# Second attention of a two-block network: values as the stationary operand, two heads in the two column halves, three outputs turned by the product itself

## The reference

```python
# 8 query heads over 2 key/value groups, three branches added with sigmoid gates
o_cmp = softmax(q @ kc.T + bias) @ vc      # 31 compressed blocks
o_slc = selected_attention(q, ks, vs, ...) # all blocks are selected at 512 tokens: full causal
o_win = banded_attention(q, kw, vw, window=512)               # causal too
o_a = g[..., 0:1] * o_cmp + g[..., 1:2] * o_slc + g[..., 2:3] * o_win
# 8 more heads over 2 groups, window 128, with a sink in the softmax
o_b = banded_attention(q_b, k_b, v_b, window=128, sinks=sinks)
x = x + concatenate([o_a, o_b], axis=-1) @ w_out
```

## Time and profile before

| | |
|---|---|
| median of 3 runs | 1645.12 us |
| span of the profiled execution | 1643.2 us |
| around its span, against the median | 1.9 us |
| second attention, first transpose to end of the output projection | some 1041 to 1271 us of the span |
| TensorE busy | 1623.6 us, 99% |
| VectorE, ScalarE, GpSimd busy | 701.2, 674.6, 759.2 us |
| granted TensorE clock | 1.00 in every stretch shown, its level of 2.4 GHz |

### The profile page before, as it was taken

The page is one execution under the profiler, slowest core; times in us unless marked ns, Lnnn a source line. Parts: engine busy times, 40 slices in busy tenths (PEclk is TensorE's granted clock), DMA queues, the critical chain, the costliest instruction groups (busy, mean ns, idle before and its releaser), DMA issues.

```text
span 1643.2 us, 21043 instructions
## 1 busy us (share of the span) xinstructions
PE 1623.6 (99%) x8100; PEld 1349.0 (82%) x8100; DVE 701.2 (43%) x1404; ACT 674.6 (41%) x1183; POOL 759.2 (46%) x581
## 2 busy tenths in 40 slices
PE   9999999999999999999999999999999999999997
PEld 7787888888888888888888888888888888888886
DVE  7276747874444227322113225555773311112224
ACT  6356645543334325422223224567563422223322
POOL 7424454564445552744445552543114544444550
PEclk9999999999999999999999999999999999999999
DMA  5411102323222231323232322212002222223221
GB/s 205 148 52 52 52 1 103 129 90 103 92 101 95 97 101 61 116 96 102 90 103 90 103 92 101 91 66 78 27 27 96 97 94 99 99 94 103 90 103 51
DMA packets 42115, 147.35 MB, mean 90 GB/s; under 512 B 4768, under 2 KB 5152, under 8 KB 42016
## 3 DMA queue, kind: packets, MB, share of 16 engines
q1 hardware_dynamic: 40680, 143.39, 25.7%
q10 hardware_dynamic: 1336, 2.63, 0.5%
HBM read 142.84 MB, written 3.41 MB: 89 GB/s over the span
## 4 chain that ended last, share of the span: by engine, by line
PE 82%; DVE 2%; issue 1%; ACT 1%; POOL 1%; DMA 0%; DVEq 0%; ACTq 0%; POOLq 0%
PE PS L587 20%; PE PS L589 20%; PE PS L588 20%; PE PS L1210 5%; PE PS L548 4%; PE PS L1221 3%; PE PS L1019 2%; PE PS L556 2%; PE PS L977 2%; PE PS L1012 1%; POOL w_lo L645 0%; DVE L L1110 0%; DMA stage<-in_weights 0%; PE PS L609 0%; ACT sq L1057 0%
## 5 line engine op out<-in xcount | busy, mean ns | idle before, releaser
L645 POOL TENSOR_TENSOR w_lo<-stage,w_hi 128x512 fp32r<-128x512 f32 x522 | 707.9, 1380 | 819.2 <-ACT w_hi L619 818.3
L619 ACT ACTIVATE w_hi<-stage 128x1024 fp32r<-128x1024 f32 x262 | 274.8, 1056 | 519.9 <-DMA stage<-in_weights 516.0
L587 PE MATMUL PS<-H_hi,w_hi 128*128 128x512 f32 x992 | 386.1, 389 | 0.4 <-DVE rcol L1407 0.4
L588 PE MATMUL PS<-H_lo,w_hi 128*128 128x512 f32 x992 | 386.0, 389 | 0.0
L589 PE MATMUL PS<-H_hi,w_lo 128*128 128x512 f32 x992 | 385.9, 389 | 0.0
L587 PEld LDWEIGHTS PS<-H_hi,w_hi 128*128 128x128 f32 x992 | 186.2, 188 | 39.0 <-DVE rcol L1407 0.7
L589 PEld LDWEIGHTS PS<-H_hi,w_lo 128*128 128x128 f32 x992 | 186.2, 188 | 38.9
L588 PEld LDWEIGHTS PS<-H_lo,w_hi 128*128 128x128 f32 x992 | 186.2, 188 | 38.7
L587 PE MATMUL PS<-A_hi,w_hi 128*128 128x512 f32 x528 | 205.6, 389 | 0.3 <-DVE A_lo L756 0.3
L589 PE MATMUL PS<-A_hi,w_lo 128*128 128x512 f32 x528 | 205.4, 389 | 0.0
L588 PE MATMUL PS<-A_lo,w_hi 128*128 128x512 f32 x528 | 205.4, 389 | 0.0
(11 more groups left out here) (234 smaller groups left out, 2048.2 us busy)
## 6 DMA issues: line engine op xcount, KB each, us to landing
stage<-in_weights SPq DMA_DIRECT2D x262, 512.0 KB, 3.2
out_t<-Y SPq DMA_DIRECT2D x8, 256.0 KB, 2.0
X<-in_x_t SPq DMA_DIRECT2D x3, 512.0 KB, 8.8
bias_line<-bias_line ACTq DMA_DIRECT2D x1, 1270.0 KB
strip<-bias_line ACTq DMA_DIRECT2D x1, 1024.0 KB, 5.0
stage<-in_weights SPq DMA_DIRECT2D x2, 256.0 KB, 4.6
V<-QF SPq DMA_DIRECT2D x4, 128.0 KB, 2.3
V<-QF SPq DMA_DIRECT2D x4, 127.8 KB, 2.4
```

The lines of the kernel that those rows point to most:

```text
L587: pe.matmul(out, a, h_hi, start=first, stop=False, skip_group_check=skip)
L588: pe.matmul(out, a, h_lo, start=False, stop=False, skip_group_check=skip)
L619: act.activation(w_hi[:, slot, :], stage[:, slot, :], ACT.Copy).then_inc(hi_done, 1)
L645: lo = pool.tensor_tensor(w_lo[:, slot, cols], stage[:, slot, cols], w_hi[:, slot, cols].bitcast(F32), ALU.subtract)
```

## The change

It concerns the second attention and its output projection only.

- The reciprocal (and the gate) multiplies the weights W before they are turned, as one `tensor_scalar` over 128 x nk in place of the 128x1 product with the gate and of the scaling of the result. The transposes of an item now wait for it.
- The values (128 keys x 64) are the stationary operand and the turned weights (128 keys x 128 queries) the moving one. The product comes out with features on the partitions; the heads of items n and n+1 go to partitions 0 to 63 and 64 to 127 of one bank, that is to the two column halves of the array. The two branches accumulate in PSUM. `soft_heads` does both heads at every odd step, two steps later than before.
- `O` becomes flat (`dve_heads_out`, `act_sum_hi` and `dve_sum_lo` for p < 4, `act_heads_hi` and `dve_heads_lo` for p >= 4): the product of four blocks of queries is copied once for each block (128x128) for p < 4, and split straight from PSUM into T_hi and T_lo for p >= 4. The 32 transposes of `O` go. The compressed branch uses the same form.
- The turned weights have four buffers instead of two, transposes two banks instead of three, the product one.
- The rows of the output projection's weights are permuted in pairs of 64, so each of its eight units is loaded by four DMAs with runs of 512 bytes in place of one.
- The filler table changes at its end, and the order of the projection's outputs.

```diff
-TURN_ORDER = [..., [0, 1, 2, 3, 4, 6, 5, 7]]
+TURN_ORDER = [..., list(range(8))]
+WO_ORDER2 = [6, 7, 0, 1, 2, 3, 4, 5]
 FILL2 = [4] * 48 + [6] * 4 + [0] + [6] * 4 + [0] + [3] * 8 + [0] + [3] * 8 + [0] + [3] * 8
-FILL2 = FILL2 + [(0, 4), 0] + [(0, 4), (3, 0)] * 5 + [(3, 12), (12, 6), 6]
+FILL2 = FILL2 + [0, 0] + [4, 3] * 5 + [1] + [6, 6, 6]
...
-                                 out=O[:, i, bass.ts(h, HD)], add=(branch == 1),
+                                 out=PS[g * HD:(g + 1) * HD, HEADS_PS, bass.ts(i, P)], add=(branch == 1),
...
-        return ITEM_PS + it.n % 3
+        return ITEM_PS + it.n % (2 if it.kind == "soft" else 3)
...
+            def soft_heads(n):
+                it = items[n]
+                if not it.add and n > 0:
+                    pe.wait_ge(a.o_done, 4 * it.group + it.i)
+                pe.wait_ge(a.wt_ready, n + 2)
+                blocks = it.nk // P
+                for kb in range(blocks):
+                    for x in (it, items[n + 1]):
+                        mm = pe.matmul(x.out, x.v[kb], turned_weights(x)[:, bass.ts(kb, P)],
+                                       start=(kb == 0 and not x.add),
+                                       stop=(kb == blocks - 1 and (x.add or x.gate is None)))
+                mm.then_inc(a.pv_done, 1)
...
-                        pe.wait_ge(a.comb if it.kind == "diff" else a.exp_done, it.exps)
-                    if it.n >= 3:
+                        pe.wait_ge(a.comb, it.exps)
+                    if it.kind == "soft":
+                        if it.n >= 2:
+                            pe.wait_ge(a.wt_ready, it.n - 1)
+                    elif it.n >= 3:
                         pe.wait_ge(a.o_done, it.n - 2)
...
-                if n >= 3:
+                if a is at2:
+                    if n >= 5 and n % 2 == 1:
+                        soft_heads(n - 5)
+                elif n >= 3:
...
                         c = link(dve.reciprocal(it.st[:, 6:7], it.st[:, 4:5]))
                         after(c)
-                        if it.gate is not None:
-                            c = link(dve.tensor_scalar(it.st[:, 6:7], it.st[:, 6:7], it.gate, None, ALU.mult))
-                            after(c)
-                        dve.sem_inc(a.comb, 1)
+                        w = W[:, it.n % 2, 0:it.nk]
+                        if it.gate is None:
+                            dve.tensor_scalar(w, w, it.st[:, 6:7], None, ALU.mult).then_inc(a.comb, 1)
+                        else:
+                            dve.tensor_scalar(w, w, it.st[:, 6:7], it.gate, ALU.mult, ALU.mult).then_inc(a.comb, 1)
...
+        def act_heads_hi(p, i, pair):
...
+                act.wait_ge(at2.pv_done, pair + 1)
...
+                act.activation(T_hi[:, p, bass.ts(i, P)], PS[:, HEADS_PS, bass.ts(i, P)], ACT.Copy).then_inc(heads_hi, 1)
...
+        def dve_heads_lo(p, i):
...
+                dve.wait_ge(heads_hi, 4 * (p - 4) + i + 1)
+                dve.tensor_tensor(T_lo[:, p, cols], PS[:, HEADS_PS, cols], T_hi[:, p, cols].bitcast(F32),
+                                  ALU.subtract).then_inc(at2.o_done, 1)
...
-                for h in (2 * pair, 2 * pair + 1):
-                    mm = pe.matmul(PS[:, 7, bass.ts(h % 2, 256)], cmp_PT(h), vc4[:, bass.ts(h // 4, 256)], start=True, stop=True)
+                for i in range(TB):
+                    for g in range(2):
+                        mm = pe.matmul(PS[g * HD:(g + 1) * HD, 7, bass.ts(i, P)], vc4[:, bass.ts(4 * g + i, HD)],
+                                       cmp_PT(4 * g + pair), start=True, stop=True)
...
+        for p in range(8):
+            for i in range(TB):
+                last = groups2[p] + (4 * i + 2 if p < 4 else 2 * i)
+                if p < 4:
+                    hook(at2, "dve", last + 6, dve_heads_out(p, i, last // 2))
+                else:
+                    hook(at2, "act0", last + 6, act_heads_hi(p, i, last // 2))
+                    hook(at2, "dve", last + 6, dve_heads_lo(p, i))
...
+            def load_by_pair(u):
+                there = stage[:, u % RING, :].rearrange("p (h j l o) -> p h j l o", h=2, j=2, l=2)
+                here = weights[ORDER[u]].rearrange("p (h g j o) -> p h g j o", h=2, g=2, j=2)
+                for g in range(2):
+                    for l in range(2):
+                        sp.dma_start(there[bass.ts(g, HD), :, :, l, :],
+                                     here[bass.ts(l, HD), :, g, :, :]).then_inc(loaded[u % RING], 16)
```

More of the change, by code:

```diff
@@ L124, in unit_order @@
     order += [U_MIX + (17 + CMP_AT[name] if name in CMP_AT else MIX_AT[name]) for name in FILL2_TASKS]
-    return order + [U_WO2 + j for j in WO_ORDER] + list(range(U_UP3, N_UNITS))
+    return order + [U_WO2 + j for j in WO_ORDER2] + list(range(U_UP3, N_UNITS))
 MIX_AT = {n: i for i, n in enumerate(("q0", "q1", "q2", "q3", "ks", "kw", "kc", "vc",
@@ L152 @@
 NAT_BANK = [4, 5, 7, 2]
-TURN_ORDER = [[c if kind == "diff" else 4 + c for kind, c in GROUPS1], [0, 1, 2, 3, 4, 6, 5, 7]]
+TURN_ORDER = [[c if kind == "diff" else 4 + c for kind, c in GROUPS1], list(range(8))]
 FILL2 = [4] * 48 + [6] * 4 + [0] + [6] * 4 + [0] + [3] * 8 + [0] + [3] * 8 + [0] + [3] * 8
-FILL2 = FILL2 + [(0, 4), 0] + [(0, 4), (3, 0)] * 5 + [(3, 12), (12, 6), 6]
+FILL2 = FILL2 + [0, 0] + [4, 3] * 5 + [1] + [6, 6, 6]
 def fill2_steps(name):
@@ L425, in build @@
         n_mix = Norm("mix", 6, "fold", X)
-        n_ffn2 = Norm("ffn2", 7, "fold", X, order=WO_ORDER)
+        n_ffn2 = Norm("ffn2", 7, "fold", X, order=WO_ORDER2)
         n_final = Norm("final", 8, "final", X)
@@ L612, in pe_token_unit, with loads_of @@
             m.then_inc(unit_done, 1)
+        def loads_of(u):
+            return u // RING + 1 + 3 * sum(1 for v in range(U_WO2, min(u + 1, U_UP3)) if v % RING == u % RING)
         def act_hi(act, u):
@@ L872, in build @@
                              v=[V[:, 0, k0 // P + kb, 2 * P + g * HD:2 * P + (g + 1) * HD] for kb in range(nk // P)],
-                             out=O[:, i, T + h * HD:T + (h + 1) * HD], add=False, gate=None,
+                             out=PS[g * HD:(g + 1) * HD, HEADS_PS, bass.ts(i, P)], add=False, gate=None,
                              sink=row[:, ROW_SINK + h:ROW_SINK + h + 1])
@@ L881, in build @@
                 it.bank = [(it.map0 + m) % 3 for m in range(len(it.maps))]
-                it.dv = it.out.shape[-1]
+                it.dv = HD if it.kind == "soft" else it.out.shape[-1]
                 it.st = stat[:, n % 4, :]
@@ L988, in ahead @@
                 return n < len(items) and n % 2 == 0 and items[n].kind == "sb" and items[n].i in (1, 2)
-            for n in range(len(items) + 3):
+            def soft_heads(n):
[10 more added lines that the diff above has]
+                mm.then_inc(a.pv_done, 1)
+            for n in range(len(items) + (4 if a is at2 else 3)):
                 f = per_item[n] if n < len(per_item) else 0
@@ L1026, in act_attn @@
             items = a.items
-            for n in range(len(items) + 2):
+            for n in range(len(items) + (6 if a is at2 else 2)):
                 for what in a.hooks["act0"].get(n, []):
@@ L1070, in dve_attn @@
             items = a.items
-            for n in range(len(items) + 4):
-                if n >= 4:
+            for n in range(len(items) + (6 if a is at2 else 4)):
+                if n >= 4 and a is at1:
                     it = items[n - 4]
@@ L1075, in dve_attn @@
                     pv = PS[:, item_bank(it), 0:it.dv]
-                    if it.kind == "soft" and it.add:
-                        dve.wait_ge(a.o_done, it.n)
-                        dve.scalar_tensor_tensor(out=it.out, in0=pv, scalar=it.st[:, 6:7], in1=it.out,
-                                                 op0=ALU.mult, op1=ALU.add).then_inc(a.o_done, 1)
-                    elif it.kind != "sb":
+                    if it.kind == "diff":
                         dve.tensor_scalar(it.out, pv, it.st[:, 6:7], None, ALU.mult).then_inc(a.o_done, 1)
@@ L1290, in pe_wo_rest @@
                 pe.wait_ge(lo_done, (U_WO, U_WO2)[b] + at + 1)
-                if WO_ORDER[at] == 3:
+                if b == 0 and WO_ORDER[at] == 3:
                     pe.wait_ge(a.o_done, 1 + max(it.n for it in a.items if item_bank(it) == 3))
                 run(pe_wo1(pe, b, at, range(6)))
-                run(pe_turn1(pe, b, at + 3))
+                if b == 0:
+                    run(pe_turn1(pe, at + 3))
             for g in (6, 7):
@@ L1671, in load @@
                         wait_unit(sp, u - RING)
-                    sp.dma_start(stage[:, u % RING, :], weights[ORDER[u]]).then_inc(loaded[u % RING], 16)
+                    if U_WO2 <= u < U_UP3:
+                        load_by_pair(u)
+                    else:
+                        sp.dma_start(stage[:, u % RING, :], weights[ORDER[u]]).then_inc(loaded[u % RING], 16)
+            def load_by_pair(u):
[5 more added lines that the diff above has]
```

(1 more changed line is left out.)

161 lines of the change are left out of this document (100 added, 61 removed).

## The result

The changed kernel took 1652.15 us (median of 4 runs, 1651.5 to 1654.31) against 1645.06 before (1644.98 to 1645.23): a ratio of 1.0045, interval 1.0033 to 1.0058. It is slower by 7.1 us where 9.3 us less were forecast, and lies above the range. Its profiled execution has a span of 1649.7 us.

The account below looks back on a forecast made before the run. The prediction took TensorE's own pace to bound the kernel. Its terms, -19.9 + 6.7 + 1.5 - 3.5 - 1.2 + 5.8 + 1.3 = -9.3 us, took 1645.1 to 1635.8 us, range 1628 to 1646.

Parts of the forecast that it names:

- The products with the values: Second attention: 432 records in 216 overlapping column-half pairs at 0.11 us, 43.7 us falling to 23.8, so 19.9 us saved.
- the changes of form: Second attention: one more switch of TensorE's array form, 48 times at 0.14 us, costing 6.7 us (4.8 to 11).
- rival (a): Products with the values: the column halves take turns, products cost 47.5 us, kernel 1655.5 us; chance 0.07.
- rival (c): Products with the values: weight loads not hidden behind matmuls in flight, 12 us more, 1647 us less some stalls; chance 0.03.
- The compressed branch: Its products with the values stay at 0.88 us each time, but two changes of form add 1.5 us.
- The transposes of O: The 32 transposes of O on TensorE go, at 0.11 us each, saving 3.5 us.
- the loads in four parts: Output projection: four DMA issues in place of one land the seventh unit later, stalling TensorE 1.3 us (0 to 4).
- the scaling ahead of its turn: Second attention: transposes of an odd item wait for VectorE's scaling; with the related stalls, 5.8 us (2 to 14).
- steps 84 and 85: Second attention: these steps have no filler to cover the wait for the scaling, costing about 1.0 us.
- The zeros of the filler table: Second attention: steps 57, 66 and 75 have no filler to cover the scaling, some 0.3 us each, 1.0 us.
- The place of GpSimd's windows: Second attention, where ScalarE waited 3.06 us for GpSimd's windows: TensorE comes earlier there, so 1.0 us more wait shows.
- Rival (b): Second attention: the VectorE and ScalarE chain binds all 48 pairs, 0.3 us more each, 1646 us, no change; chance 0.11.

Follow-up runs that it names:

- The later logits: Against the changed kernel, TensorE's logits of a pair stand behind the step's first filler and the scaling of the item two before; scaling stays in SBUF: 1661.1 us.

## Why the prediction was wrong

It placed TensorE as the bound and asked whether the other engines could follow: the right question, answered wrongly for one instruction.

- **The products with the values** were forecast at -19.9 with full overlap, and the changes of form at +6.7, together -13.2. Measured by starts, the value records fall from 47.1 to 30.8 us, and the filler ahead of each of 48 groups stands 0.10 us longer (1071.96 to 1072.29 above, 0.33 for 0.227), so about -11.5. The mechanism was right, and rival (a), turns, and rival (c), loads unhidden, fell: a pair costs 0.11 us. The compressed branch, forecast at +1.5, measured about +1.7 by starts.
- **The transposes of O** (-3.5) measured -3.4; the loads in four parts (+1.3) about +1.8; steps 84 and 85 (1.0) showed a wait of 1.2 us.
- **The failed step is the scaling ahead of its turn**, +5.8 on record, bounds 2 and 14. Taking the scaling away gave 16.7 us, and the kernel without it still has 5.0 us of waits at its place in the order, which belong to the same term: some 22 us, an estimate from the two. The forecast less its 5.8 would be 1630.0 for that kernel, and it took 1635.49.
- **What the term lacked: GpSimd**, 10.3 us, of which 0.9 are waits for w_lo. The price per instruction, 0.29 us, came from a row without GpSimd beside it. That row is of the very form that can be held up, and cheaper than this one even alone (0.41 us for 256 columns with a factor and a gate). The earlier trace rows has GpSimd busy 29.4 of 69 us in the same stage, and the prediction used that column for nothing.
- **What the term had too small**: its own length, with the windows, 6.3 us, and the order, 5.0. The zeros of the filler table were counted at steps 57, 66 and 75; the one at step 52 was left out, and TensorE waits 1.1 us there. The place of GpSimd's windows was put at 1.0 and has 1.5 without the scaling, 3.5 with it. Even without GpSimd's subtractions the kernel took 1641.8 us, 6.0 above the forecast, so GpSimd is the largest part of the miss and not all of it.
- **The range** was narrower than its own terms. The bad ends on record (changes of form 11, scaling 14, loads 4), with the other terms as forecast, add up to +5.9, which is 1651.0 and not 1645; the good ends give 1628.8. The measured 1652.15 lies above even that.
- **Rival (b)**, the chain in all pairs, named the right chain, but not its places. The waits of this kernel stand at 18 places and not in all 48 pairs; the longest, 3.5 us, is at the windows, and 1.6 us stand at item 59, where the scaling had its usual 0.48 us but stood behind work of the compressed branch in VectorE's queue. The later logits cost 9 us, at eight places and in good part through a wait of their own, so they don't price this chain.
- **The clock** was not in the sum at all: behind the 3.5 us wait it was 0.50 for 2.7 us in which TensorE had work, which is some 1.3 us lost, an estimate (it is part of the 16.7).

What the bounds lacked was a rival of this kind: the same row, scaled while GpSimd runs, up to one instruction of GpSimd longer (1.3 us for 512 columns).

## What to carry to other kernels

When an edit puts a VectorE instruction with all operands in SBUF on the critical chain, look at which engine is busy at that moment, not only at the instruction's time alone: a tensor_scalar at doubled pace waited for GpSimd's running instruction, one that read PSUM or wrote its sum didn't. A group whose mean doesn't grow with its size, or whose longest is several times its shortest, is probably being held, and the engine whose end it shares is the one to look at. A wait behind it may have begun earlier, though: here ten of eighteen were for a scaling of usual length. Where the chain is tight, the slower form that never waits can be worth more than the faster one (eight instructions gave 4.65 us).

## What the runs showed of the hardware

- VectorE's tensor_scalar from SBUF to SBUF took 0.35, 0.41, 0.48 and 0.55 us for 128 to 512 columns alone (with two factors), and up to 1.82 beside GpSimd; from PSUM 0.41, 0.54, 0.68 and 0.81, beside GpSimd or not; with its sum 0.35, 0.48, 0.62 and 0.75. A step of two columns changed nothing.
- GpSimd's subtraction took 475 ns for 128 columns, 756 for 256 and 1.3 us for 512: some 0.2 us for each instruction, an estimate from the differences.
- Two column halves of 64 stationary and 128 moving columns run side by side (16 records in 1.03 us), and overlap over three or four records even if one half's records are all queued ahead of the other's.
- After 3.5 us without work TensorE's matmuls of 512 columns started 0.43 us apart at first, half of the usual pace, with a granted clock of 0.50.
